# One wide matmul for the high and the low part in three long output projections

## The reference, cut to what matters

```python
def conv_ffn(h, w_in, conv_w, conv_b, w_out):      # two of them, D_FF = 2816
    z = causal_dwconv(h @ w_in, conv_w, conv_b)
    u, g = jnp.split(z, 2, axis=-1)
    return (jax.nn.gelu(g) * u) @ w_out            # 2816 x 1024
...
x = x + conv_ffn(h, ffn_w_in[l], ffn_conv_w[l], ffn_conv_b[l], ffn_w_out[l])
...
x = x + gt2 * (jnp.square(jax.nn.relu(h @ ffn_w1[l])) @ ffn_w2[l])   # 4096 x 1024
return rms_norm_2(x, final_g)
```

## Time and profile before

| what | value |
|---|---|
| median of 3 runs | 1096.98 us (1096.81 to 1097.29) |
| profiled execution | 1095.12 us, of which the span of its instructions is 1093.3 us |
| TensorE matmuls busy | 1048.6 us, 8608 of them |
| VectorE busy | 837.0 us |
| ScalarE busy | 630.7 us |
| matmuls of the three projections | 3 x 608 |

### The profile page before, as it was taken

How to read it: one execution, slowest core, us unless ns; L and a number is a source line. 1 busy time by engine, 2 the same in 40 slices (tenths; PEclk the granted TensorE clock), 3 DMA queues, 4 the chain that set the end, 5 groups by cost and what they waited for, 6 DMA issues and landing times.

```text
span 1093.3 us, 20978 instructions
## 1 busy us (share of the span) xinstructions
PE 1048.6 (96%) x8608; PEld 993.7 (91%) x8608; DVE 837.0 (77%) x1433; ACT 630.7 (58%) x1059; POOL 65.5 (6%) x79
## 2 busy tenths in 40 slices
PE   8999899999989989999999997999999989999996
PEld 7876899999988888999999897899989989999996
DVE  6466999888798878988788789998965597755452
ACT  7545686666567856766665693222333367976440
POOL 1222100000002001000001000000000021000010
PEclk9999999999999999999999999999999999999999
DMA  9358366566667854767776542222435275566651
GB/s 357 117 188 312 126 223 193 193 181 192 196 213 230 283 200 160 264 216 254 249 218 200 186 159 92 64 90 90 144 93 163 61 264 176 194 192 193 194 171 39
DMA packets 59424, 200.41 MB, mean 183 GB/s; under 512 B 6720, under 2 KB 10432, under 8 KB 59200
## 3 DMA queue, kind: packets, MB, share of 16 engines
q1 hardware_dynamic: 57600, 194.54, 54.7%
q10 hardware_dynamic: 1728, 4.53, 1.2%
HBM read 197.99 MB, written 1.05 MB: 182 GB/s over the span
## 4 chain that ended last, share of the span: by engine, by line
PE 79%; DVE 12%; ACT 5%; DMA 2%; issue 1%; ACTq 0%; POOL 0%; SPq 0%; DVEq 0%
PE ps L480 78%; DVE wlo L1575 4%; ACT L1050 1%; ACT whi L1050 1%; DVE rst L1608 1%; ACT hh L1050 1%; DMA ring<-pa_w_out 1%; DVE x L1575 1%; DVE hl L1581 1%; DVE w L1575 1%; DMA ring<-rg_w_out 1%; DMA ring<-pa_w_in 0%; DMA ring<-w_o 0%; DVE raw L1575 0%; DVE bks L1575 0%
## 5 line engine op out<-in xcount | busy, mean ns | idle before, releaser
L480 PE MATMUL ps<-hh,whi 128*128 128x256 f32 (+1 forms) x1656 | 473.6, 286 | 6.2 <-DVE wlo L1575 3.2
L480 PE MATMUL ps<-hl,whi 128*128 128x256 f32 (+1 forms) x1656 | 462.9, 280 | 0.0
L480 PE MATMUL ps<-hh,wlo 128*128 128x256 f32 (+1 forms) x1656 | 462.8, 279 | 0.0
L1575 DVE TENSOR_TENSOR wlo<-ring,whi 128x1024 fp32r<-128x1024 f32 (+2 forms) x314 | 376.2, 1214 | 54.5 <-ACT whi L1050 53.9
L1050 ACT ACTIVATE whi<-ring 128x1024 fp32r<-128x1024 f32 (+2 forms) x314 | 322.4, 1038 | 65.5 <-PE ps L480 44.8
L480 PEld LDWEIGHTS ps<-hh,whi 128*128 128x128 f32 x1656 | 314.9, 190 | 27.4 <-issue 15.6
L480 PEld LDWEIGHTS ps<-hl,whi 128*128 128x128 f32 x1656 | 315.1, 190 | 1.3 <-issue 1.0
L480 PEld LDWEIGHTS ps<-hh,wlo 128*128 128x128 f32 x1656 | 315.2, 190 | 0.0
L480 PE MATMUL ps<-hidh,whi 128*128 128x256 f32 x608 | 168.1, 276 | 0.0
L480 PE MATMUL ps<-hidh,wlo 128*128 128x256 f32 x608 | 167.9, 276 | 0.0
L480 PE MATMUL ps<-hidl,whi 128*128 128x256 f32 x608 | 167.9, 276 | 0.0
(11 more groups left out here) (364 smaller groups left out, 1325.7 us busy)
## 6 DMA issues: line engine op xcount, KB each, us to landing
ring<-ffn_w_in SPq DMA_DIRECT2D x88, 512.0 KB, 3.5
ring<-ffn_w SPq DMA_DIRECT2D x64, 512.0 KB, 4.6
ring<-w_in SPq DMA_DIRECT2D x51, 512.0 KB, 3.4
ring<-ada_w SPq DMA_DIRECT2D x48, 512.0 KB, 4.1
ring<-ffn_w_out SPq DMA_DIRECT2D x32, 448.0 KB, 3.4
ring<-rg_w_in SPq DMA_DIRECT2D x20, 512.0 KB, 4.6
ring<-ffn_w_out SPq DMA_DIRECT2D x16, 512.0 KB, 3.6
ring<-pa_w_in SPq DMA_DIRECT2D x15, 512.0 KB, 6.8
```

Of the source, the lines that this page charges most:

```text
L480: return e.matmul(o, l, r, start=start, stop=stop)
L1575: return e.tensor_tensor(o, a, b, op)
```

## The change

High and low part of the hidden activations become the two halves of one tile, with the low part 22 (or 32) tiles behind the high part. In the three long projections one matmul reads both halves, 512 columns, and writes all 512 columns of the PSUM bank: the first half collects high weight by high activation, the second half high weight by low activation. The third matmul (low weight by high activation) adds into the first half as before. So there are two matmuls and two weight loads for each k in place of three. VectorE then adds both halves to `x`, first the second half, then, once that is done, the first half.

```diff
-        hidh = [alloc(st, "hidh", [128, 22, T], F32R)] * 2
-        hidl = [alloc(st, "hidl", [128, 22, T], F32R)] * 2
+        hid = [alloc(st, "hid", [128, 2, 22, T], F32R)] * 2
...
-        hid2h = alloc(st, "hidh2", [128, 32, T], F32R)
-        hid2l = alloc(st, "hidl2", [128, 32, T], F32R)
+        hid2 = alloc(st, "hid2", [128, 2, 32, T], F32R)
+        hid2h, hid2l = hid2[:, 0, :, :], hid2[:, 1, :, :]
...
+            def long_linear(w, m, both, nk, need):
+
+                p = take((w, m))
+                wide = p[:, :].rearrange("p (a t) -> p a t", a=2)
+                for c, k, n in chunks(w, m, nk):
+                    low.wait_ge(e, c)
+                    j = turn[c] % NS
+                    for q in range(n):
+                        need(k + q)
+                        mm(wide, whi[j][:, q, :], both[:, :, k + q, :], k + q == 0, False)
+                        t = mm(p[:, 0:T], wlo[c % NR][:, q, :], both[:, 0, k + q, :], False, k + q == nk - 1)
+                    t.then_inc(*through.up(c))
...
-                    linear(w, ms, of, nk, need, rows)
+                    if nk > 8:
+                        long_linear(w, ms[0], of, nk, need)
+                    else:
+                        linear(w, ms, of, nk, need, rows)
...
-            def add_to_x(n, m, p):
+            def add_to_x(n, m, p, corrections=None):
+                if corrections is not None:
+                    if n < 5:
+                        tt(x[:, m, :], corrections, x[:, m, :], ADD).then_inc(*resid.up((n, m, "corrections")))
+                    else:
+                        stt(x[:, m, :], corrections, mod[:, 40 + m:41 + m], x[:, m, :], MUL, ADD).then_inc(*resid.up((n, m, "corrections")))
+                    resid.wait_ge(e)
...
-                        add_to_x(n, m, out_of(w, m, nk))
+                        add_to_x(n, m, out_of(w, m, nk), ps[where[w, m]][:, T:2 * T] if nk > 8 else None)
```

More of the change, by code:

```diff
@@ L313, in build @@
         alloc(st, "fill", [128, 112])
-        hidh[1] = alloc(st, "hidh", [128, 22, T], F32R)
-        hidl[1] = alloc(st, "hidl", [128, 22, T], F32R)
+        hid[1] = alloc(st, "hid", [128, 2, 22, T], F32R)
+        hidh, hidl = [a[:, 0, :, :] for a in hid], [a[:, 1, :, :] for a in hid]
         zu[1] = alloc(st, "zu", [128, 3, T])
@@ L715, in also @@
                     mod_turn()
-                residual(2 * l + 2, f"ffn_w_out{l}", 22, pair(hidh[l], hidl[l]), lambda k: ff_dve.wait_ge(e, (l, "lo", k)), also)
+                residual(2 * l + 2, f"ffn_w_out{l}", 22, hid[l], lambda k: ff_dve.wait_ge(e, (l, "lo", k)), also)
             def rglru():
@@ L1033, in tensor_program @@
             relu_ffn()
-            residual(6, "ffn_w2", 32, pair(hid2h, hid2l), lambda k: ff_dve.wait_ge(e, (2, "lo", k)))
+            residual(6, "ffn_w2", 32, hid2, lambda k: ff_dve.wait_ge(e, (2, "lo", k)))
             stats(6)
```

## The result

The kernel became slower: 1104.98 us as the median of 4 runs (1103.29 to 1106.6), against 1096.89 us (1096.79 to 1097.29) for the kernel before, on the same chip. The ratio is 1.0077, with a 95% interval of 1.0045 to 1.0109. The forecast was 1097.1 us, and its range ended at 1100.8. The profiled execution took 1105.62 us, of which the span is 1103.8 us, 10.5 more than the span of before.

What follows compares the result with a forecast made beforehand. TensorE's 113.3 ns step was taken to bound the projections wherever the path runs through it, VectorE and ScalarE elsewhere; +1.8, +0.1 and -1.8 us made +0.1, hence 1097.1 us, range 1094.2 to 1100.8.

Steps and rivals of the forecast that it cites:

- the size of the wide matmul: Long projections: 512-column matmul predicted at 215.8 ns in place of 226.7, taken from a plain float32 record.
- s: TensorE's predicted saving per k in the three long projections: 9 ns, from 340 to 331 ns.
- The lower bound of s: Long projections: -4.5 ns, a narrow matmul at 117.8 ns beside a wide one of twice 113.3.
- a step that costs by its columns alone has s = 0: Working for the bounds in the projections: if only columns set TensorE's step, the merged matmul saves nothing per k.
- the third rival: TensorE's pace elsewhere may be 113.3 or 117.8 ns: 1.2 us per 30 us, either sign; included in the forecast's 0.62.
- The Trainium skill's rule: Warm matmul gap, columns over 2.4 GHz plus about 2.5 ns; by it a saving of 2.5 ns and 1100.1 us.
- The path: VectorE leads from column 3 in the first projection, late in the second; TensorE leads the third: +1.8, +0.1, -1.8 us.
- the forecast's own formula: Whole kernel: 4.2 us of additions less 0.454 us for each ns of s, break-even at s = 9.
- The additions: 24 new VectorE instructions, 0.45 us each in the first two projections, 0.51 in the third; 4.2 us on the path.
- the second load was the bound: First rival, projections: narrow matmul's load hidden behind the wide one, s up to 16, -3.1 us, 1093.9 us; chance 0.15.
- the load was hidden anyway: Second rival, projections: columns set the step, s is 0 or little more, +4.2 us, 1101.2 us; chance 0.22.
- a pair takes 338 ns or more: Stated condition for being wrong: wide and narrow matmul together at 338 ns or more, against some 331 forecast.

Runs made afterwards that it cites:

- adds_only: Changed kernel with three 256-column matmuls per k again, VectorE still adding both halves; ratio 1.0031 (0.9985 to 1.0077) against the kernel before, k at 340.0 ns.
- m1_forms: Small separate kernel running each matmul form in its own series; three narrow took 360 ns a k, the pair 353.2 apart and 346.7 side by side.
- adjacent: Changed kernel with high and low part of each k side by side, read as one 512-column piece; 1107.13 us, ratio 1.0112, 353.3 ns a k.
- m2_places: Small separate kernel with weights at 16 places, 32 bytes apart; three narrow took 340.0 to 360.1 ns a k, the pair 346.6 to 353.7.
- m3_two_places: Small separate kernel with high and low weights at 8 places each; the pair took 346.5 to 353.8 ns a k, three narrow 340.0 to 373.

## Why the prediction was wrong

**The step that failed is the size of the wide matmul**: "The other row is plain float32 of 256 columns", "I read each as one load with 512 streamed columns", "By this the wide matmul takes 215.8 ns in place of 226.7". It measured 235 ns. With the neighbour at 118.3 (117 was in the working) a k is 353.3 ns in place of 331, and s is -13.3 ns instead of +9. The lower bound of s, -4.5 (344.5 ns a k), was too high as well: it gave the slower rhythm to one of the three parts, and the measured pace is the slower rhythm for all three (3 x 117.8 = 353.4).

**"a step that costs by its columns alone has s = 0"** was the second thought behind the bounds, and it left out that before stood on the favourable side. I took 113.3 ns as what a step costs, and the wide one as something to be built from it. The runs show that 113.3 is the pace of one position and of one way in (340.0 or 353.3 ns a k at the same addresses), which the pair did not reach at any position. The earlier trace rows had it: 117.8 ns in another stage. I used it as a correction of a few ns on the narrow matmul and as the third rival, "30 us of it are 1.2 us, of either sign; alone it leaves the time within 0.2%". It was the case that came, over the whole of three projections and always to the slow side.

**The Trainium skill's rule** ("TensorE: Matmul & The Clock Gate", section "Back-to-back issue gap", columns over 2.4 GHz and 2.5 ns) gives 215.8 ns for 512 columns as an estimate; no run here shows it for fp32r, where the wide matmul took 226.7 to 235. The section gives this rule for an isolated matmul, which the prediction's sentence on it leaves out.

**The path was right, and so was the sum's form.** TensorE was slower, so it set the pace up to column 3 of the first projection, where I had VectorE late from there on: the addition at 276.65 us starts 0.02 us after TensorE's part of the chain has ended (261.78 + 14.85). Thus 88 k count there: 88 x 13.3 = 1.2 us and five additions of 0.45, 3.4 in all, where 3.45 was measured. In the third 256 x 13.3 = 3.4 us and 0.5 for the addition, 3.9, where 3.84 was measured. In the second 132 x 13.3 = 1.8 and 1.3 for three additions make 3.1, and 2.42 was measured; adds_only too shows 0.72 us there and not 1.3. The chain of before, then that of after, shows where the rest went:

```profile
613.04 0.40 ACT cosT L1050
...
616.49 1.28 ACT L1050
```

```profile
618.91 0.40 ACT cosT L1065
...
621.71 1.28 ACT L1065
```

Counted from the projection's first matmul (550.53 and 553.33 us), the first row comes 3.08 us later in after, which is the 3.1. From there to ScalarE's next function table it is 3.45 us in before and 2.80 in after (and in adds_only). In between ScalarE issues five transfers, and the first of them comes 1.15 us behind the first row in before and 0.51 in after. So 0.65 us of the lateness are absorbed between these two rows, where the prediction passed the additions on in full. Why the transfers came later in before is not shown. By the forecast's own formula, 4.2 - 0.454 x (-13.3) is 10.2 us, and the span grew by 10.5. That this is so near is partly luck: the second stage is 0.7 us short of its sum, and 0.8 us of the 10.5 arose outside the three stages. (The medians differ by 8.1 us. The profiled execution of before was 1.8 us under its median, that of after 0.6 above.)

**The additions**: 0.45 us each and 0.51 in the third projection were right (0.88 and 1.00 us for two). Their 4.2 us on the path measured 3.6. After against adds_only is 1.10, 1.70 and 3.34 us in the three stages, 6.1 us for the wide matmul; 454 x 13.3 is 6.0.

**The rivals.** That the second load was the bound fell: the loads now have idle time and the k is longer. That the load was hidden anyway had the sign, 1101.2 us, and m1_forms bears out half of it: columns cost 0.42 ns each and the load is not what ends last. It had no place for a loss on TensorE. Of the conditions under which I said I would be wrong, "a pair takes 338 ns or more" is the one that came; "a wide read of two pieces 22 tiles apart has a cost of its own" did not (adjacent). Transfers and banks were no matter, as said: adds_only has the same tile and the same halves at 340.0 ns.

**What stays open.** What in the chip makes a position fast, why the narrow form has two paces at the same one, and why the pair has only the slow one there is not settled. The pair isn't free of this elsewhere: with 0 bytes between activations and weights, side by side, it took 346.7 ns in m1_forms and 353.5 in m2_places, and m2_places and m3_two_places tried one way in for each place. So that no place brings the pair to 340 holds for the ways in that were tried. I can say where each pace occurs and not why. Nor is it settled how much of the scatter between executions comes from such stages: the profiled ones differ by some 4 us in the one from 140 to 245 us, and for the others there are only total times.

## What to carry to other kernels

A merged matmul saves its load only where the load ends last; read first whether the step follows the columns or the load, and take the price of the new form from a row of the same type and the same neighbours, never from another type's record. Where a long row of matmuls runs at the best pace that any of its stages shows, treat that pace as something that can be lost: price the new form by the slower pace for all of its parts before asking for a gain of a few ns a step. And when a bench and the kernel disagree on the same instructions, compare their addresses before their instructions.

## What the runs showed of the hardware that I had not expected

- With fp32r and a load of 128 columns before each matmul, the pace depends on the position of the weights against the moving operand, with near the same values 256 bytes on: 113.3 to 120 ns for 256 columns alone, 226.7 to 234.3 for 512, and 340 to 360 ns for three narrow with both weights at one place. Moving the activations by 32 bytes in the large kernel cost 16 ns a k (340.0 to 356.0) in the narrow form and gained 6.7 (353.3 to 346.7) in the wide one.
- At one position the narrow form has two steady paces, 340.0 and 353.3 ns a k. A single matmul of 64 columns ahead gave the first, one of 96 the second, and neither was left in the 24 k that followed. In the large kernel a stage of some 900 matmuls ran at 113.0 ns in one execution and at 117.6 in another, from the same program.
- A matmul of 512 columns is no cheaper for each column than one of 256 at the best position: 235 or 226.7 ns against twice 113.3.
